# Layer one's attention reordered: bias rows ahead of x, dots in groups of four, weight splits ahead of query heads, value blocks in another order

## What is computed

```python
q_lat, c_kv, q_idx, k_idx, w_idx = split(h @ w_in)      # 16 heads x 128, 128, 8 x 64, 64, 8
c_kv = rms_norm(c_kv, latent_g)
dots = einsum('bqjd,bsd->bqjs', q_idx, k_idx) * 64**-0.5
score = einsum('bqj,bqjs->bqs', w_idx, relu(dots))      # causal; the 128 best keys of each query are kept
logits = q_lat . c_kv[kept] * 128**-0.5 + rel_bias[bucket(t - s)]
o = einsum('bthr,hrd->bthd', softmax(logits) @ c_kv[kept], w_uv) @ w_out
```

## Time and profile before

| | us |
|---|---|
| median of 3 runs (lowest to highest) | 1185.35 (1185.19 to 1185.37) |
| the profiled execution | 1187.02 |
| its span, first to last instruction | 1185.2 |
| TensorE busy | 1160.8 (98%) |
| GpSimd busy | 610.3 (51%) |
| VectorE busy | 530.6 (45%) |
| ScalarE busy | 458.2 (39%) |

### The profile page before, as it was taken

How to read it: one execution, slowest core, us unless ns; L and a number is a source line. 1 busy time by engine, 2 the same in 40 slices (tenths; PEclk the granted TensorE clock), 3 DMA queues, 4 the chain that set the end, 5 groups by cost and what they waited for, 6 DMA issues and landing times.

```text
span 1185.2 us, 16084 instructions
## 1 busy us (share of the span) xinstructions
PE 1160.8 (98%) x5666; PEld 965.0 (81%) x5666; DVE 530.6 (45%) x931; ACT 458.2 (39%) x854; POOL 610.3 (51%) x359
## 2 busy tenths in 40 slices
PE   7999999999999999999999999899999999999997
PEld 5767889988888888888888878888888888888887
DVE  5379867644544444441111376644444344420001
ACT  5343257763422322233222376644323322322332
POOL 4335847765444544544444588834445445534441
PEclk9999999999999999999999999999999999999999
DMA  7441411114333233224442342313332333223331
GB/s 212 172 137 44 152 27 46 47 44 123 91 106 95 82 106 106 81 74 125 132 140 67 102 106 54 80 38 106 107 99 78 106 106 87 79 82 90 97 97 71
DMA packets 181572, 112.46 MB, mean 95 GB/s; under 512 B 7340, under 2 KB 175591, under 8 KB 181528
## 3 DMA queue, kind: packets, MB, share of 16 engines
q1 hardware_dynamic: 180800, 110.68, 32.5%
q10 hardware_dynamic: 728, 1.22, 0.3%
HBM read 109.72 MB, written 8.45 MB: 100 GB/s over the span
## 4 chain that ended last, share of the span: by engine, by line
PE 91%; DVE 3%; issue 1%; ACT 1%; POOL 0%; DVEq 0%; ACTq 0%
PE ps L602 29%; PE ps L604 28%; PE ps L603 28%; PE ps L611 2%; PE ps L817 1%; DVE work L1607 1%; PE ps L993 1%; PE ps L796 1%; DVE work L1591 1%; PE ps L996 0%; DVE xs_lo L1494 0%; DVE std L1612 0%; PE ps L888 0%; PE ps L650 0%; DVE w_lo L1494 0%
## 5 line engine op out<-in xcount | busy, mean ns | idle before, releaser
L493 POOL TENSOR_TENSOR w_lo<-raw,w_hi 128x1024 fp32r<-128x1024 f32 (+1 forms) x198 | 454.8, 2318 | 487.4 <-ACT w_hi L1119 478.8
L602 PE MATMUL ps<-xs_hi,w_hi 128*128 128x512 f32 (+3 forms) x1024 | 398.8, 389 | 3.5 <-POOL w_lo L493 2.1
L604 PE MATMUL ps<-xs_hi,w_lo 128*128 128x512 f32 (+3 forms) x1024 | 394.7, 385 | 0.0
L603 PE MATMUL ps<-xs_lo,w_hi 128*128 128x512 f32 (+3 forms) x1024 | 394.6, 385 | 0.0
L1119 ACT CAST w_hi<-raw 128x1024 fp32r<-128x1024 f32 (+1 forms) x194 | 176.9, 961 | 432.0 <-PE ps L604 431.8
L602 PEld LDWEIGHTS ps<-xs_hi,w_hi 128*128 128x128 f32 x1024 | 192.6, 188 | 47.4 <-issue 3.4
L603 PEld LDWEIGHTS ps<-xs_lo,w_hi 128*128 128x128 f32 x1024 | 192.5, 188 | 39.2 <-issue 1.1
L604 PEld LDWEIGHTS ps<-xs_hi,w_lo 128*128 128x128 f32 x1024 | 192.4, 188 | 38.6
L602 PE MATMUL ps<-act_hi,w_hi 128*128 128x512 f32 (+1 forms) x374 | 143.0, 382 | 0.0
L604 PE MATMUL ps<-act_hi,w_lo 128*128 128x512 f32 (+1 forms) x374 | 141.7, 379 | 0.0
L603 PE MATMUL ps<-act_lo,w_hi 128*128 128x512 f32 (+1 forms) x374 | 140.4, 375 | 0.0
(11 more groups left out here) (191 smaller groups left out, 1352.1 us busy)
## 6 DMA issues: line engine op xcount, KB each, us to landing
raw<-in_ffn_w_gate_up SPq DMA_DIRECT2D x88, 512.0 KB, 4.8
raw<-in_ffn_w_down SPq DMA_DIRECT2D x32, 384.0 KB, 3.6
raw<-in_a_w_in SPq DMA_DIRECT2D x20, 512.0 KB, 4.9
raw<-in_ffn_w_down SPq DMA_DIRECT2D x32, 320.0 KB, 4.1
bias_toep<-bias_row SPq DMA_DIRECT2D x4, 1024.0 KB
toep<-bias_toep SPq DMA_DIRECT2D x16, 256.0 KB, 2.7
raw<-in_a_w_out SPq DMA_DIRECT2D x8, 512.0 KB, 4.4
raw<-in_b_w_in SPq DMA_DIRECT2D x8, 512.0 KB, 5.3
```

The source lines that it names most:

```text
L493: nc.gpsimd.tensor_tensor(pieces(w_lo, n)[half], pieces(raw, n)[half], pieces(w_hi, n)[half].bitcast(F32), ALU.subtract)\
L602: nc.tensor.matmul(dst, wh, xh, start=start, stop=False, **kw)
L603: nc.tensor.matmul(dst, wh, xl, start=False, stop=False, **kw)
L604: return nc.tensor.matmul(dst, wl, xh, start=False, stop=stop, **kw)
```

## The change

- **Start.** The parameter rows' DMA moves from ScalarE's queue to SP's, behind the identity and ahead of x. ScalarE's queue begins with `hot` and `rel_sb` and has x behind them. On TensorE the two bias matmuls come before both halves of x; the first no longer waits for the parameters. VectorE copies g_sb before it works on x.
- **Seam.** Slab 2's first tile goes to bank 5 and ahead of the keys' matmul; the second goes to bank 0.
- **Dots.** Two pairs of dots follow each other, then four steps of the query tile. In the first block two steps of the query tile come ahead of all dots and three behind each group.
- **Split order.** ScalarE: after q_head(2) the splits of slabs 6 and 7, then heads 3 to 6, then slab 8, and on as before. GpSimd: slab 5, heads 0 to 2, slab 6, uv_lo, slab 7, heads 3 to 6, slab 8, and on.
- **Values.** The second four values go in the order 1, 0, 2, 3 (`V_BLOCK`). turn(0) waits for each bank by itself, weigh(0) and weigh(1) for the last two. On ScalarE q_head(15) comes behind the copies of values 4 to 7.

```diff
+V_BLOCK = (0, 1, 2, 3, 1, 0, 2, 3)
...
             sp.dma_start(tab[:, 0:P], consts[:, 0:P]).then_inc(id_in, 16)
+            sp.dma_start(par_rows[:, :], par_in).then_inc(small_in, 16)
             x_part(0)
...
             split_lo(S_A2 + 2)
             for h in range(3):
                 q_part(h)
-            for i in range(1, 6):
+            split_lo(S_A2 + 3)
+
+            pool.wait_ge(uvh_done, 1)
+            nc.gpsimd.tensor_tensor(uv_lo[:, :, :], uv_raw[:, :, :], uv_hi[:, :, :].bitcast(F32),
+                                    ALU.subtract).then_inc(uvl_done, 1)
+            split_lo(S_A2 + 4)
+            for h in range(3, 7):
+                q_part(h)
+            for i in range(3, 6):
                 split_lo(S_A2 + 2 + i)
                 q_part(2 * i + 1)
                 q_part(2 * i + 2)
...
             nc.tensor.transpose(ps[:, 7, 0:59], par_rows[:, :], ident[0:59, 0:59]).then_inc(par_t, 1)
-            x_turn(0)
-
             pe.wait_ge(hot_in, 32)
             pe.wait_ge(rel_one, 1)
 
+            nc.tensor.matmul(ps[0:H, 6, :], rel_sb[:, :], hot[:, 0:T], start=True, stop=True).then_inc(g_mm, 1)
+
             pe.wait_ge(par_done, 1)
-            nc.tensor.matmul(ps[0:H, 6, :], rel_sb[:, :], hot[:, 0:T], start=True, stop=True).then_inc(g_mm, 1)
             nc.tensor.matmul(ps[0:H, 7, 0:GLEN - T], rel_sb[:, :], hot[:, T:GLEN], start=True, stop=True).then_inc(g_mm, 1)
+            x_turn(0)
             x_turn(1)
...
             tile(ps[:, 3, :], 1, 0, P, 256, xh, xl)
+
+            tile(ps[:, 5, :], 2, 0, 0, 256, xh, xl)
 
             pe.wait_ge(kw_done, 2)
...
             pe.wait_ge(craw_done, 1)
-            tile(ps[:, 0, :], 2, 0, 0, 256, xh, xl)
-            tile(ps[:, 1, :], 2, 0, P, 256, xh, xl)
+            tile(ps[:, 0, :], 2, 0, P, 256, xh, xl)
...
+                lead = 2 if i == 1 else 0
+                if lead:
+                    query(range(0, lead))
+                dots_two(0)
+                dots_two(2)
+                query(range(lead, 4 + lead // 2))
+                dots_two(4)
+                dots_two(6)
+                query(range(4 + lead // 2, DM)).then_inc(unit_done, 1)
...
-                s, h0 = j % 4, 8 * (j // 4)
+                s, h0 = V_BLOCK[j], 8 * (j // 4)
...
-                    pe.wait_ge(av_l, j - 3)
+                    pe.wait_ge(av_l, s + 1)
...
             def turn(h):
-                if h == 0:
-                    pe.wait_ge(av_l, 8)
-                    pe.wait_ge(qa_done, H + 2)
                 for s in (2, 3, 1, 0):
                     b, c0 = ((3, 0), (4, 0), (5, 0), (5, 2 * P))[s]
+                    if h == 0 and s == 2:
+                        pe.wait_ge(av_l, 5)
+                    if h == 0 and s == 1:
+                        pe.wait_ge(av_l, 6)
+                    if h == 0 and s == 0:
+                        pe.wait_ge(qa_done, H + 2)
...
                 pe.wait_ge(ptl_done, 3 * h + 3)
+                if h < 2:
+                    pe.wait_ge(av_l, 7 + h)
...
-            act.dma_start(par_rows[:, :], par_in).then_inc(small_in, 16)
+            act.dma_start(hot[:, :], consts[0:BUCKETS + 1, C_HOT:C_END]).then_inc(hot_in, 16)
+            act.dma_start(rel_sb[0:BUCKETS, :], rel_bias).then_inc(hot_in, 16)
...
             q_head(2)
-            for i in range(5):
+            split_after(S_A2 + 1)
+            split_after(S_A2 + 2)
+            for h in range(3, 7):
+                q_head(h)
+            for i in range(2, 5):
                 split_after(S_A2 + 1 + i)
...
             exponents(1)
-            q_head(H - 1)
             for j in range(4, 8):
                 value_hi(j)
+            q_head(H - 1)
```

More of the change, by code:

```diff
@@ L535, in _ @@
                 q_part(2 * i + 2)
[L536 to L539, removed]
             for h in range(13, H - 1):
@@ L705, in _, with dots_two @@
                 pe.wait_ge(lo_done, 2 * n + 2)
-                for j in range(0, JI, 2):
+                def dots_two(j):
                     d = h * JI + j
@@ L710, in _ @@
                         pe.wait_ge(relu_done, d - 2)
-                    if d < 4:
+                    else:
                         pe.wait_ge(qi_l, d + 2)
@@ L719, in _, with query @@
                             [ki_hi[q, 0:n_keys] for q in r], [ki_lo[q, 0:n_keys] for q in r]).then_inc(dots, 2)
-                    for k in (j, j + 1):
+                def query(ks):
+                    for k in ks:
                         c = k * 256 + (h % 2) * P
@@ L723, in _ @@
                                    xh(k), xl(k), k == 0, k == DM - 1)
-                last.then_inc(unit_done, 1)
+                    return last
+                lead = 2 if i == 1 else 0
[7 more added lines that the diff above has]
+                query(range(4 + lead // 2, DM)).then_inc(unit_done, 1)
             pe.wait_ge(csq_done, 1)
@@ L1159, in _ @@
                     act.dma_start(x_tok[:, t, c], x_in[0, t * P:(t + 1) * P, c]).then_inc(x_in_s[half], 16)
-                if half == 0:
-                    act.dma_start(hot[:, :], consts[0:BUCKETS + 1, C_HOT:C_END]).then_inc(hot_in, 16)
-                    act.dma_start(rel_sb[0:BUCKETS, :], rel_bias).then_inc(hot_in, 16)
             act.wait_ge(set_up, 4)
@@ L1191, in _ @@
                 act.wait_ge(unit_done, u + 5)
-                nc.scalar.copy(qi_hi[:, 2 + u, :], ps[:, u, :]).then_inc(qi_h, 1)
+                nc.scalar.copy(qi_hi[:, 2 + u, :], ps[:, (5, 0)[u], :]).then_inc(qi_h, 1)
             split_after(2)
@@ L1528, in _ @@
             dve.wait_ge(par_done, 1)
+            dve.wait_ge(g_mm, 2)
+            nc.vector.tensor_copy(g_sb[:, 0:T], ps[0:H, 6, :]).then_inc(g_done, 1)
+            nc.vector.tensor_copy(g_sb[:, T:GLEN], ps[0:H, 7, 0:GLEN - T]).then_inc(g_done, 1)
             for m in range(DM):
@@ L1537, in _ @@
                 nc.vector.tensor_copy(x[:, m, :], ps[:, m, :]).then_inc(x_new, 1)
[L1538 to L1542, removed]
             dve.wait_ge(set_up, 3)
@@ L1564, in _ @@
                 dve.wait_ge(qi_h, u + 1)
-                lo_part(qi_lo[:, u, :], ps[:, (2, 3, 0, 1)[u], :], qi_hi[:, u, :].bitcast(F32), qi_l)
+                lo_part(qi_lo[:, u, :], ps[:, (2, 3, 5, 0)[u], :], qi_hi[:, u, :].bitcast(F32), qi_l)
             def q_scale(h, bank, par):
```

## The result

The changed kernel takes 1179.65 us (median of 5 runs, 1179.10 to 1180.98), the kernel before 1185.35 (5 runs beside it, 1184.73 to 1186.82). The ratio is 0.9939, with a 95% interval of 0.9922 to 0.9955: 5.7 us faster. The forecast was 1179.6, its sum -5.65. The profiled execution took 1179.65 as well (span 1177.8); that of the kernel before took 1187.02, 1.7 above its median, so the two traces differ by 7.4 us and the medians by 5.7.

The account below looks back on a forecast made before the run. TensorE, busy 98% of the span, bounds the kernel, so only its idle time or work pays. Terms -1.8 + 0.8 - 1.5 - 2.3 - 0.85 = -5.65 from profiled 1187.02, less 1.67 to the median's scale: 1179.6 us, range 1176.6 to 1182.6.

Parts of the forecast that it names:

- Part 1: Start: bias matmuls run while TensorE waits for x, first tile near 15.9 instead of 18.3; 1.8 us faster (0 to 2.8).
- the clock's: Start: 2.4 us more tile work may run at half rate, costing 0 to 1.2 us; middle 0.6 taken.
- the early gain is lost: Rival, 18%: at the start hot or x lands later and the clock rises late, gain only 0.2; 1181.2 us.
- Part 2: Seam at 42 us: 0.87 saved before the keys' matmul, 1.7 waited for slab 3's split; 0.8 us slower.
- the seam doesn't stall: Rival, 10%: at the 42 us seam ScalarE's split falls earlier than read, so no wait; 1178.0 us.
- Part 3: Indexer dots: four half-height form changes saved at 0.39 each, third block counted at nothing; 1.5 us faster (0 to 2.3).
- Part 4: Split order: earlier GpSimd splits remove TensorE's weight slab wait at 114 us; 2.3 us faster (0 to 2.4).
- a new stall replaces the one at 114: Rival, 12%: the next slab, behind q_head(6), or the early one comes late; price up to 2.3, 1182.0 us.
- the one on the slower side: Rival, 4%: GpSimd's moved splits block VectorE's top-k rounds, q_scale(3) up to 7.1 us later; 1186.8 us.
- the narrow reading: Moved GpSimd splits: the port lock holds only for two-input VectorE operations, so nothing is added to top-k rounds.
- Part 5: Values near 170 us: turn(0) wait of 1.84 removed, turn(1) about 1.0 late; 0.85 us faster (0 to 1.84).
- The gains before 106 are eaten by top-k: Rival, 6%: top-k's chain starts no earlier, and one more term fails; about 1184 us.

Follow-up runs that it names:

- the start alone: Kernel before with only the start's change (bias rows ahead of x, parameter rows on SP's queue, hot and rel_sb first on ScalarE's): 1184.99 us, ratio 0.9982.
- the old order on the new queues: Kernel after with its DMA queues, but x's first half ahead of the bias matmuls again and VectorE's bias copies behind x's second piece: 1181.06 us, ratio 0.9948.
- old-queues kernel: Kernel after with TensorE's new order, but par_rows first on ScalarE's queue and hot and rel_sb behind x's first half: 1183.21 us, ratio 0.9964.
- undone kernel: Kernel after with one part reversed: slab 2's first tile behind the keys' matmul again, 1179.32 us; or, separately, old value order, turn(0) wait and q_head(15) place, 1180.02 us.
- the dots alone: Kernel before with only the regrouped dots (groups of four, two query tile steps ahead in block one): 1185.30 us, ratio 0.9976.
- the split order alone: Kernel before with only slabs 6 and 7 split ahead of query heads 3 to 6, on GpSimd and ScalarE: 1184.16 us, ratio 0.9968.
- ineffective warm-up: Kernel after with both new waits removed, plus two unused fp32 matmuls on zeros before the parameter rows come: 1177.86 us, ratio 0.9915.

## Why the prediction was right, step by step

**Part 1 (forecast 1.8, bounds 0 to 2.8): right in direction, mis-sized in the traces.** The first tile stands where the sum put it, 15.9, but by two errors that cancel: the landing of x (13.7, forecast 12.6) and the transposes (1.97 us, forecast 3.33). The term that failed is the clock's, +0.6 as the middle between nothing and 1.2: it measured -0.8. The matmuls of the first tile run at full rate from the second on, so part 1 is worth 3.2 us between the two traces, outside my bounds. I had let the rate rise either with the tiles or at the old moment, and not thought of its coming earlier. All nine profiles with the bias first show full rate by the first tile; the five with the old order, the kernel before twice among them, show it only 1.4 to 2.2 us into the tiles. In the median the start alone gave 2.0; its profiled execution gave 3.3 and lost 1.5 of it to the fall of the clock behind the wait at 110. How often a start is slow, and whether the order always decides it, can't be told from one profile per kernel; the spread of the old order on the new queues speaks against "always".

That hot would land in time was the choice on which the rival "the early gain is lost" hung. It did: TensorE starts the bias at 5.50. The old-queues kernel shows the other side: bias at 8.43, and a first tile at 18.15 and not 18.32, nearly nothing gained, as the prediction had reckoned for that case (0.1).

**Part 2 (forecast 0.8 slower): right.** Wait at 52.83 for GpSimd's w_lo, 1.71 lost where I had 1.7, 0.87 saved; 0.67 net by the undone kernel. The rival that the seam doesn't stall is refuted by the row.

**Part 3 (1.5): right.** A change of form costs 0.40 (forecast 0.39); 1.35 with the dots alone, 1.5 in the full change. The third block gives nothing, as forecast: it is taken by the waits at 79.54 and 102.19. One step was wrong: "no new wait" for the relu. There is one of 0.36 us, but it stands ahead of the q_odd wait, where VectorE's chain sets the time in any case.

**Part 4 (2.3): right.** 2.48 with the split order alone, no new wait behind it. The rival "a new stall replaces the one at 114" fell. So did the one on the slower side: rounds of top-k stay 3.16 us apart beside 11.8 us of GpSimd's work. That was the narrow reading. In the Trainium skill (SBUF — State Buffer, Who interferes with whom) an operation of VectorE with at most one input in SBUF, outside the two-port modes, doesn't contend with GpSimd. The trace agrees: MAX8 took 1.48 us for three beside GpSimd's work, as without it.

**Part 5 (0.85): right.** 1.00 by the undone kernel, with the wait in turn(1) at 167.3 to 168.2 for GpSimd that was forecast.

The sum in the traces is -3.2 + 0.8 - 1.5 - 2.5 - 1.0 = -7.4; in the medians -5.7, and the forecast was -5.65. That the forecast came so near is in part luck. Two misses cancel. Against the trace my sum was 1.75 too small, 1.4 of it in the clock term of part 1. And the profiled execution of before stood 1.67 above its median, while that of after is its median: I took the 1.67 off both sides. Some of it may be the half-rate start (0.8), which the change removed; then part 1 is worth less in a typical execution than between these two traces. The medians leave 1.5 for it (5.7 without the 4.2 of the other parts), and the start alone gave 2.0, so 1.8 isn't refuted there. This is inferred, not tested. The median of before is itself loose: 1185.35 beside the change, 1186.94 to 1187.45 in the later sessions.

"The gains before 106 are eaten by top-k" (1184) fell as well: the gain stood at 3.94 at the third block's first dots (73.12 to 69.18) and at 3.91 at the q_odd wait.

The best version run here is the change with both new waits removed: 1178.51, and 1177.86 with the ineffective warm-up. Two operations moved give 2.3 us more by the trace, 1.1 by the medians, which come from different sessions.

## What to carry to other kernels

When a wait is removed by moving work ahead of it, ask at once what the same engines owe next: here the seam gave back twice the 0.87 it saved and the values nearly half of their 1.84. Both waits could be placed and sized from the trace of before, and both went when one operation each was moved. A change of matmul form into half height and back cost 0.4 us per visit here, so group them, but only where TensorE isn't waiting for another engine's chain anyway. And at a start, look at where a small transfer stands in its queue: the 2 KB of rel_sb, issued behind x, landed at 8.4 us and held everything behind; issued ahead of x, they were there by 5.5.

## What the runs showed that I had not expected

- The granted clock in the windows reads 1.00 from 14 to 20 us of the kernel before, while its tiles there start 0.43 us apart. At a start the distance between matmuls has to be read, not that column.
- Transposes, bias matmuls and four passes of a matmul on zeros from 1.48 us on left TensorE at 1.2 GHz to the end of x's first half or nearly (13.1 us in the kernel after), in some profiles into the second half (2.53 and 2.77 us for its transposes and not 1.97); what brings the rise is open.
- A wait of 2.15 us was followed by a fall to 1.2 GHz that cost 1.5 us in one execution, the start alone; the same wait (2.13 to 2.17) in the profiles of the kernel before, twice, and of the dots alone was not. The kernel before spreads over 4.0 to 5.8 us within a session of nine or more runs, with a group near 1190; the kernels without that wait over 1.4 to 3.0 us, except the old order on the new queues (5.2). Of the two other kernels with the wait the dots alone spread over 5.9 us, but the start alone over only 2.9, with twelve runs each. That the wait makes the group near 1190 is therefore a guess, not shown.
- A similar fall in layer two, between 748 and 762 us and worth about 1.6 us, came in the profiles of six kernels and not in the other eight, with no relation to the part of the change that I can see. TensorE's waits there, 1.9 and 1.1 us for VectorE, are the same in the kernels before and after, which have no fall, as in the seam undone and the dots alone, which have it. Before two traces are compared over their whole length it has to be taken out.
